# First output products ahead of the last transposes, three banks ahead of the last wait, and a last norm by column sums in five pieces

## The reference

```python
def rms_norm_2(x, g):
    xf = x.astype(jnp.float32)
    y = xf * lax.rsqrt(jnp.mean(xf * xf, axis=-1, keepdims=True) + RMS_EPS)
    return (y * g.astype(jnp.float32)).astype(x.dtype)

def conv_ffn(xn, w_gate, conv_w, conv_b, w_up, w_down):
    ...
    h = jax.nn.gelu(gc, approximate=False) * (xn @ w_up)
    return h @ w_down

    for i in range(DEPTH_2):                      # 2 layers
        hn = rms_norm_2(h, norm_mix[i])
        ...                                       # moba (0) or latent (1) attention
        mix = ...(attention output).reshape(B, S, H * dh) @ w_o
        h = h + mix
        f = conv_ffn(rms_norm_2(h, norm_ffn[i]), ...)
        h = h + f
    return rms_norm_2(h, norm_final)
```

## Time and profile before

| | |
|---|---|
| median of 3 runs | 1183.01 us (1180.21 to 1183.13) |
| the profiled execution's own time | 1181.99 us |
| its span, first to last instruction | 1180.2 us |
| TensorE busy | 1144.6 us, 97% of the span |
| VectorE busy | 903.1 us, 77% |
| ScalarE busy | 684.1 us, 58% |
| chain that ended last | TensorE 90%, VectorE 4%, ScalarE 2%, DMA 1% |
| TensorE's granted clock, mean | 0.991 of 2.4 GHz |
| weight stream | 188.7 MB read, 161 GB/s over the span |

### The profile page before, as it was taken

The page is one execution under the profiler, slowest core; times in us unless marked ns, Lnnn a source line. Parts: engine busy times, 40 slices in busy tenths (PEclk is TensorE's granted clock), DMA queues, the critical chain, the costliest instruction groups (busy, mean ns, idle before and its releaser), DMA issues.

```text
span 1180.2 us, 25357 instructions
## 1 busy us (share of the span) xinstructions
PE 1144.6 (97%) x9641; PEld 1112.2 (94%) x9641; DVE 903.1 (77%) x1555; ACT 684.1 (58%) x1200; POOL 10.2 (1%) x13
## 2 busy tenths in 40 slices
PE   6999999999999999999999999999999999999996
PEld 6999999989899999999899899999998889999995
DVE  5788878678687998888687668777777767877775
ACT  6768764445546666665654456555566746655552
POOL 1000000000001000000000000000000000000000
PEclk9998999999999999999999999999999999999998
DMA  7665645521263777665543246666643423766660
GB/s 240 203 215 164 189 130 161 163 72 56 72 187 111 220 217 211 193 195 183 171 149 108 73 126 224 210 193 194 195 151 118 127 82 116 232 213 195 190 184 36
DMA packets 52779, 190.82 MB, mean 162 GB/s; under 512 B 5984, under 2 KB 5984, under 8 KB 52704
## 3 DMA queue, kind: packets, MB, share of 16 engines
q1 hardware_dynamic: 52416, 188.77, 52.0%
q10 hardware_dynamic: 288, 0.99, 0.2%
HBM read 188.69 MB, written 1.05 MB: 161 GB/s over the span
## 4 chain that ended last, share of the span: by engine, by line
PE 90%; DVE 4%; ACT 2%; DMA 1%; issue 1%; SPq 0%; DVEq 0%; ACTq 0%
PE bank L603 26%; PE bank L604 25%; PE bank L605 25%; PE bank L611 2%; PE bank L613 1%; PE bank L612 1%; DMA w_raw<-weight_stream 1%; PE bank L740 1%; DVE w_low L1661 1%; PE bank L754 1%; PE bank L753 1%; PE bank L752 1%; PE bank L726 1%; PE bank L724 1%; ACT w_high L1226 1%
## 5 line engine op out<-in xcount | busy, mean ns | idle before, releaser
L1661 DVE TENSOR_TENSOR w_low<-w_raw,w_high 128x1024 fp32r<-128x1024 f32 x356 | 434.2, 1223 | 150.1 <-ACT w_high L1226 147.4
L1226 ACT ACTIVATE w_high<-w_raw 128x1024 fp32r<-128x1024 f32 x356 | 375.2, 1058 | 268.6 <-PE bank L605 193.1
L603 PE MATMUL bank<-h_high,w_high 128*128 128x256 f32 x1760 | 495.6, 282 | 10.6 <-DVE h_low L1699 10.4
L604 PE MATMUL bank<-h_low,w_high 128*128 128x256 f32 x1760 | 489.0, 278 | 0.0
L605 PE MATMUL bank<-h_high,w_low 128*128 128x256 f32 x1760 | 488.9, 278 | 0.0
L603 PEld LDWEIGHTS bank<-h_high,w_high 128*128 128x128 f32 x1760 | 332.3, 189 | 12.0 <-issue 9.8
L604 PEld LDWEIGHTS bank<-h_low,w_high 128*128 128x128 f32 x1760 | 333.0, 189 | 0.4
L605 PEld LDWEIGHTS bank<-h_high,w_low 128*128 128x128 f32 x1760 | 331.7, 188 | 0.0
L603 PE MATMUL bank<-r_high,w_high 128*128 128x256 f32 x942 | 265.9, 282 | 3.9 <-ACT arena L1615 2.1
L604 PE MATMUL bank<-r_low,w_high 128*128 128x256 f32 x942 | 262.4, 279 | 0.0
L605 PE MATMUL bank<-r_high,w_low 128*128 128x256 f32 x942 | 262.2, 278 | 0.0
(11 more groups left out here) (211 smaller groups left out, 1127.0 us busy)
## 6 DMA issues: line engine op xcount, KB each, us to landing
w_raw<-weight_stream SPq DMA_DIRECT2D x356, 512.0 KB, 4.2
x<-x_in SPq DMA_DIRECT2D x4, 256.0 KB, 5.8
out<-arena SPq DMA_DIRECT2D x4, 256.0 KB, 2.3
small<-small_in ACTq DMA_DIRECT2D x1, 937.5 KB, 8.9
small<-small_in ACTq DMA_DIRECT2D x1, 30.5 KB, 4.0
```

The costliest lines, as they stand in the source:

```text
L603: mm(out_ap, wh, high, start=start, stop=False, skip_group_check=True)
L604: mm(out_ap, wh, low, start=False, stop=False, skip_group_check=True)
L1226: fn(w_high[:, c % RING, :], w_raw[:, c % RAW, :], ACT.Copy).then_inc(high_ready, 1)
L1661: v.tensor_tensor(w_low[:, c % RING, :], w_raw[:, c % RAW, :], f(w_high[:, c % RING, :]), ALU.subtract).then_inc(low_ready, 1)
```

## The change

Four edits, in one diff.

1. At the end of each of the three attentions, a part of the output projection that needs only the first pair moves ahead of the transposes of pair 3. For `wo1` and `wo2` these are the products of chunk 0 on `acc` banks 0, 2 and 3 (`free=(0, 2, 3)`), 18 matmuls; bank 1 (PSUM bank 5) still holds the attention's last group, and its 6 products stand behind the transposes. For `ao` (`output_tiles`) they are the first 6 matmuls of tile 0; behind the transposes come tile 0's columns 2 to 5, tile 1's columns 0 to 5, and then both tiles' last two columns, which need pair 3. On VectorE the subtraction of pair 0 (`output_low(ends, (0,))`) moves ahead of the normalisation of the last group; in the first attention the other three pairs also move ahead of the scaling of the last merge gate.
2. At the end of each feed forward the last but one chunk is taken on three banks instead of two before the wait for the last hidden tile.
3. The last norm: `x` is added and squared in pieces of 2, 2, 2, 1 and 1 feature tiles. Each squared piece is multiplied on TensorE as the stationary operand by a column of ones, so that the sums lie with tokens on the partitions, 128x2 in all; ScalarE's root and VectorE's reciprocal are of 128x2; TensorE spreads the result back to 128x256 by two products with the identity. ScalarE multiplies `x` by the norm's weight meanwhile, and VectorE multiplies the result by the spread roots, five multiplications instead of eight. The table for the root is loaded on ScalarE ahead of the squares.
4. Five stores instead of four: SP issues the first four (3 of 256 KB, one of 128 KB), ScalarE the last (128 KB).

```diff
-            for p in range(4):
-                sp.wait_ge(norm_ready, p + 1)
-                sp.dma_start(out[:, 2 * p:2 * p + 2, :], pieces(x_norm, p)).then_inc(out_stored, 16)
-            sp.wait_ge(out_stored, 64)
+            for n, (k, size) in enumerate(LAST_PIECES[:-1]):
+                sp.wait_ge(norm_ready, n + 1)
+                sp.dma_start(out[:, k:k + size, :], x_norm[:, k:k + size, :]).then_inc(out_stored, 16)
+            sp.wait_ge(out_stored, 16 * len(LAST_PIECES))
...
+                    if k == 0 and inside:
+                        for p in free:
+                            rows_of_bank(BASE[stage], p, high[:, 0, :], low[:, 0, :], True, False)
+                        inside()
+                        for p in range(4):
+                            if p not in free:
+                                ins = rows_of_bank(BASE[stage], p, high[:, 0, :], low[:, 0, :], True, False)
+                        ins.then_inc(chunk_used, 1)
...
+            def output_tiles():
+
+                first = BASE["ao"]
+                chunk_here(first + 1)
+                banks = [tile_bank(TILE0["ao"] + i)[:, 0:S] for i in range(2)]
+                for i, some in ((0, range(2)), (0, range(2, 6)), (1, range(6)), (0, (6, 7)), (1, (6, 7))):
+                    for k in some:
+                        if i == 0:
+                            turned(0)(k)
+                        ins = split_product(banks[i], first + i, k * P, r_high[:, k, :], r_low[:, k, :],
+                                            k == 0, k == DT - 1)
+                        if k == DT - 1:
+                            ins.then_inc(chunk_used, 1)
+                    if some == range(2):
+                        turn_output(0, o0, (3,))
+                column_tiles("ao", r_high, r_low, first=2)
...
-                for pair in ((0, 1), (2,), (3,)):
+                for pair in ((0, 1, 2), (3,)):
...
-            turn_output(1, o1, (3,))
-            output_projection("wo1", r_high, r_low, turned(1))
+            output_projection("wo1", r_high, r_low, turned(1), free=(0, 2, 3), inside=lambda: turn_output(1, o1, (3,)))
...
-            norm_sums(6)
+            for n, (k, size) in enumerate(LAST_PIECES):
+                pe.wait_ge(x_squared, 4 * 6 + n + 1)
+                for m in range(k, k + size):
+                    for t in range(TT):
+                        ins = mm(bank[2][:, t:t + 1], squares[:, m, t * P:(t + 1) * P], ones,
+                                 start=m == 0 and t == 0, stop=m == DT - 1, skip_group_check=True)
+            ins.then_inc(sumsq_ready, 1)
+            pe.wait_ge(rstd_ready, 6 + 1)
+            for t in range(TT):
+                ins = mm(bank[3][:, t * P:(t + 1) * P], rstd_col[:, t:t + 1].to_broadcast([P, P]), ident,
+                         start=True, stop=True)
+            ins.then_inc(norm_spread, 1)
...
-            norm(6)
-            roots(6)
+            def squared(n):
+                k, size = LAST_PIECES[n]
+                act.wait_ge(acc_read, 4 * ACC_FFN2 + n + 1)
+                fn(squares[:, k:k + size, :], x[:, k:k + size, :], ACT.Square).then_inc(x_squared, 1)
+
+            def weighted(p):
+                for k in (2 * p, 2 * p + 1):
+                    ins = fn(x_norm[:, k, :], x[:, k, :], ACT.Identity, scale=par("norm", 6 * DT + k, 1))
+                ins.then_inc(out_scaled, 1)
+
+            fn(stats[:, 6:7], eps_col, ACT.Sqrt)
+            squared(0)
+            squared(1)
+            weighted(0)
+            for n in range(2, len(LAST_PIECES)):
+                squared(n)
+            act.wait_ge(sumsq_ready, 6 + 1)
+            fn(std_col, bank[2][:, 0:TT], ACT.Sqrt, bias=eps_col, scale=1.0 / D).then_inc(std_ready, 1)
+            for p in range(1, 4):
+                weighted(p)
+            act.wait_ge(norm_ready, len(LAST_PIECES))
+            act.dma_start(out[:, DT - 1:DT, :], x_norm[:, DT - 1:DT, :]).then_inc(out_stored, 16)
...
+                    if i == count + 2:
+                        output_low(ends, (0,))
                     if i >= 3 and i % 4 == 2:
                         output((i - 3) // 4)
...
             attention(0, 2 * NH, o0, probs_t0, gated=True, before=merge_gate, after=merge_split)
+            output_low(0, (1, 2, 3))
             merge_gate(2 * NH + 3)
-            output_low(0)
...
+            for n, (k, size) in enumerate(LAST_PIECES):
+                acc_bank_done(dve, 6, k // 2)
+                src = acc[k // 2][:, k % 2 * S:(k % 2 + size) * S].rearrange("p (k t) -> p k t", k=size)
+                v.tensor_tensor(x[:, k:k + size, :], src, x[:, k:k + size, :], ALU.add).then_inc(acc_read, 1)
+            dve.wait_ge(std_ready, 6 + 1)
+            v.reciprocal(rstd_col, std_col).then_inc(rstd_ready, 1)
+            dve.wait_ge(norm_spread, 1)
+            for n, (k, size) in enumerate(LAST_PIECES):
+                dve.wait_ge(out_scaled, k // 2 + 1)
+                v.tensor_tensor(x_norm[:, k:k + size, :], x_norm[:, k:k + size, :],
+                                bank[3][:, 0:S].unsqueeze(1).to_broadcast([P, size, S]),
+                                ALU.mult).then_inc(norm_ready, 1)
```

More of the change, by code:

```diff
@@ L321, in build @@
         norm_ready = sem("norm_ready")
+        out_scaled = sem("outputs_scaled_by_weights")
+        norm_spread = sem("last_norm_spread")
         h_high_ready = sem("h_high_ready")
@@ L518, in sum_banks @@
             return a[:, 0:S], b[:, 0:TT]
+        LAST_PIECES = [(0, 2), (2, 2), (4, 2), (6, 1), (7, 1)]
         def pieces(ap, p):
@@ L634, in two_tiles, with column_tiles @@
                             ins.then_inc(chunk_used, 1)
-            def column_tiles(stage, high, low, h_wait=None, after=None, inside=None, norm=None):
+            def column_tiles(stage, high, low, h_wait=None, after=None, inside=None, norm=None, first=0):
                 if norm is not None:
@@ L641, in column_tiles @@
                     norm_sums(norm)
-                for i in range(0 if norm is None else 2, SIZE[stage]):
+                for i in range(first if norm is None else 2, SIZE[stage]):
                     c = BASE[stage] + i
@@ L667, in row_chunk, with output_projection @@
                 ins.then_inc(chunk_used, 1)
-            def output_projection(stage, high, low, h_wait=None):
+            def output_projection(stage, high, low, h_wait=None, free=(), inside=None):
                 for k in range(DT - LATE):
@@ L674, in output_projection @@
                         h_wait(k)
-                    row_chunk(BASE[stage] + k, high[:, k, :], low[:, k, :], first=k == 0)
+                    if k == 0 and inside:
[6 more added lines that the diff above has]
+                        ins.then_inc(chunk_used, 1)
+                    else:
+                        row_chunk(BASE[stage] + k, high[:, k, :], low[:, k, :], first=k == 0)
                 chunk_here(BASE[stage] + DT - 1)
@@ L1038, in _ @@
                       last=lambda: turn_output(0, o0, range(3)), pairs=True)
-            turn_output(0, o0, (3,))
-            column_tiles("ao", r_high, r_low, turned(0))
+            output_tiles()
             pe.wait_ge(mg_scaled, 16)
@@ L1207, in _ @@
                       last=lambda: turn_output(2, o2, range(3)))
-            turn_output(2, o2, (3,))
-            output_projection("wo2", r_high, r_low, turned(2))
+            output_projection("wo2", r_high, r_low, turned(2), free=(0, 2, 3), inside=lambda: turn_output(2, o2, (3,)))
             feed_forward(2, ACC_FFN2)
-            norm_sums(6)
+            for n, (k, size) in enumerate(LAST_PIECES):
[10 more added lines that the diff above has]
+            ins.then_inc(norm_spread, 1)
         @block.scalar
@@ L1723, in attention @@
             def attention(n, count, o, probs_t, gated=False, before=None, after=None, use=ALL_BANKS, filled=0):
-                done = NH * n
+                done, ends = NH * n, 0 if gated else n - 1
                 def row_max(i):
@@ L1769, in attention, with output_low @@
                         after(i)
-            def output_low(n):
-                for p in range(DT // 2):
+            def output_low(n, pairs):
+                for p in pairs:
                     low(pieces(r_low, p), bank[p][:, :].rearrange("p (k t) -> p k t", k=2), pieces(r_high, p),
@@ L2131, in _ @@
                       after=lambda i: rope(i + QK_AHEAD - 1) if i + QK_AHEAD <= SIZE["qk1"] else None, use=BLOCK_BANKS)
-            output_low(1)
+            output_low(1, (1, 2, 3))
             stage("wo1", lambda i: None, count=DT - LATE)
@@ L2213, in _ @@
                       filled=NH - QUERIES_AHEAD)
-            output_low(2)
+            output_low(2, (1, 2, 3))
             stage("wo2", lambda i: None, count=DT - LATE)
@@ L2218, in _ @@
             feed_forward(2)
-            norm(6)
-            inverse_roots(6)
-            for k in range(DT):
```

(6 more changed lines are left out.)

## The result

| | before | after |
|---|---|---|
| median of 5 runs each, in turn on one chip | 1181.13 us (1180.21 to 1183.13) | 1174.83 us (1172.98 to 1176.11) |
| ratio | | 0.9942, 95% interval [0.9929, 0.9954] |
| span of the profiled execution | 1180.2 us | 1173.1 us |
| from the last wide product's start to the span's end | 12.74 us | 10.80 us |

The changed kernel is 0.58% faster, 6.9 us of 1181 (5.4 to 8.4); the two medians by themselves lie 6.3 apart. Two more rounds of the same kernel gave 0.9934 [0.9911, 0.9956] and 0.994 [0.992, 0.9961]. The total is near the forecast, but its parts are not: the sum lacks a term of about 2 us for the distance of products in the projections, and its term for the kernel's end is about 1 us too large. The two partly cancel.

A forecast was written before the change was run, and what follows sets the result against it. TensorE, busy 97% of the span, bounds the kernel; only its waits and the work after its last product can be won. 1.05 + 1.10 + 1.10 (attentions) + 0.1 (feed forwards) + 2.65 (end) = 6.0 us: 1183.01 to 1177.0, range 1174.6 to 1180.3.

The forecast's parts named there:

- its term for the kernel's end: Last norm and stores: narrow column sums, two-column root and reciprocal, five multiplications; the end was to come 2.65 us earlier.
- The section of the Trainium skill named above: For the last norm's column sums, "LDWEIGHTS (loading the stationary operand)": 107 ns per 128-column load, making 3.4 us instead of 3.2.

## What to carry to other kernels

Before comparing two profiles, take the distance of equal matmuls, start to start, in each stage: if it differs with the clock and the work the same, that difference is not the edit's wait and may not come back in the next execution; compare stages at equal levels, and take two or three profiles of the unchanged kernel. Fill a wait with work that needs only what is already there, and check that the engine behind the wait had a moment to spare. Price many tiny matmuls by their distance start to start, and a drain of stores by the mean of its slices, not by the best; work on TensorE behind a pause or a row of narrow matmuls has to be priced at both clocks.

## What the runs showed that was not expected

- Products of 128x256 have two distances at granted clock 1.00, 0.1133 and 0.1178 us, 4% apart. Each is kept through 240 to 432 matmuls, and in the stretches followed here it changed only behind matmuls of another kind: four transposes left 20 of 22 stretches low, a single one 4 of 4 high, and the feed forwards behind the norms were always low. Over the three projections that is up to 3.85 us, 0.33% of the kernel.
- Matmuls of one column stood 0.112 us a record apart, as far as products of 256 columns at the low level, and 0.213 at half the clock. The section of the Trainium skill named above has a load of 128 columns take 107 ns; the trace agrees to 5%.
- The clock fell not only behind a wait of 3.06 us but also inside an unbroken row of one-column matmuls, from 1.00 to 0.57 and 0.50 within two microseconds, in some executions and not in others of the same program.
- Five stores from SP alone landed in 2.1 to 2.2 us each, where with the last one on ScalarE's queue the five took 2.4 to 2.8. The two kernels also cut the output differently, so the queue isn't shown to be the cause.
